# Where four small column sums stand in the first up projection of a transformer kernel

## The reference

```python
mod = silu(c) @ w_ada + b_ada                       # 6 * 1024 numbers
shift1, scale1, gate1, shift2, scale2, gate2 = split(mod, 6)
h = rms_norm(x, g_norm1) * (1 + scale1) + shift1
x = x + (1 + gate1) * (mixers(h) @ w_out)
h2 = rms_norm(x, g_norm2) * (1 + scale2) + shift2
u = causal_depthwise_conv(h2 @ w_up, w_conv, b_conv)    # w_up: 1024 x 5632, 3 taps
val, gte = split(u, 2)
x = x + (1 + gate2) * ((val * silu(gte)) @ w_down)      # w_down: 2816 x 1024
```

## Time and profile before

| | |
|---|---|
| median of 3 runs | 1052.29 us (1052.28 to 1053.61) |
| span of the profiled execution, first to last instruction | 1051.3 us |
| PE busy | 1020.2 us (97%) |
| DVE busy | 733.6 us (70%) |
| ACT busy | 562.0 us (53%) |
| share of PE in the chain that ended last | 87% |
| granted TensorE clock, mean | 0.997 of full speed |

### The profile page before, as it was taken

One profiled execution on the slowest core, in us unless ns is written; L12 is line 12 of the kernel. 1 busy time (PEld: TensorE's weight loads), 2 busy tenths in 40 slices (PEclk: granted clock), 3 DMA queues, 4 the chain that ended last, 5 costly groups with the idle time before them and its releaser, 6 DMA issues.

```text
span 1051.3 us, 22984 instructions
## 1 busy us (share of the span) xinstructions
PE 1020.2 (97%) x10004; PEld 966.9 (92%) x10004; DVE 733.6 (70%) x1194; ACT 562.0 (53%) x858; POOL 0.9 (0%) x7
## 2 busy tenths in 40 slices
PE   7999999999999999998999999999999999999996
PEld 6898889999999998986879999999888799999996
DVE  3898677899976667888557566566857665565654
ACT  4456474665565548764236444454667654444541
POOL 0000000000000000000000000000000000000000
PEclk9999999999999999999999999999999999999999
DMA  9978465466645553331005555465224435554541
GB/s 350 398 259 310 172 239 186 176 239 242 229 139 193 203 231 121 126 118 43 4 6 196 199 174 190 140 214 209 101 78 166 170 124 201 191 175 158 194 166 41
DMA packets 31236, 185.82 MB, mean 177 GB/s; under 512 B 3472, under 2 KB 4768, under 8 KB 13984
## 3 DMA queue, kind: packets, MB, share of 16 engines
q1 hardware_dynamic: 31136, 184.36, 49.2%
HBM read 183.29 MB, written 1.05 MB: 175 GB/s over the span
## 4 chain that ended last, share of the span: by engine, by line
PE 87%; DVE 5%; DMA 3%; ACT 3%; issue 1%; SPq 1%; DVEq 0%; ACTq 0%
PE banks L383 47%; PE banks L1390 17%; PE banks L348 3%; PE banks L380 2%; PE banks L660 1%; DMA land<-in_mkv_a 1%; DVE wlo L328 1%; PE banks L1933 1%; PE banks L1574 1%; PE banks L595 1%; PE banks L1923 1%; ACT whi L313 1%; PE banks L663 1%; DMA raw<-in_a_in 1%; DMA raw<-in_w_in 1%
## 5 line engine op out<-in xcount | busy, mean ns | idle before, releaser
L328 DVE TENSOR_TENSOR wlo<-raw,whi 128x2048 fp32r<-128x2048 f32 (+3 forms) x163 | 323.0, 1982 | 169.3 <-ACT whi L313 169.1
L313 ACT ACTIVATE whi<-raw 128x2048 fp32r<-128x2048 f32 (+3 forms) x163 | 270.7, 1663 | 107.4 <-PE banks L1390 73.5
L383 PE MATMUL banks<-h_lo,whi 128*128 128x256 f32 x1376 | 175.1, 279 | 0.0
L383 PE MATMUL banks<-h_hi,wlo 128*128 128x256 f32 x1376 | 173.1, 277 | 0.0
L383 PE MATMUL banks<-h_hi,whi 128*128 128x256 f32 x1360 | 172.1, 279 | 0.1
L383 PEld LDWEIGHTS banks<-h_lo,whi 128*128 128x128 f32 x1376 | 163.9, 187 | 3.2 <-issue 2.6
L383 PEld LDWEIGHTS banks<-h_hi,wlo 128*128 128x128 f32 x1376 | 163.8, 187 | 1.5 <-issue 1.2
L383 PEld LDWEIGHTS banks<-h_hi,whi 128*128 128x128 f32 x1360 | 162.1, 187 | 2.3 <-issue 1.2
L1416 ACT ACTIVATE u<-u 128x256 f32<-128x256 f32 x44 | 18.4, 418 | 124.9 <-DVE u L1470 124.9
L1390 PE MATMUL banks<-m_lo,whi 128*128 128x256 f32 x528 | 73.4, 278 | 0.0
L1390 PE MATMUL banks<-m_hi,wlo 128*128 128x256 f32 x528 | 73.2, 277 | 0.0
(11 more groups left out here) (453 smaller groups left out, 1408.8 us busy)
## 6 DMA issues: line engine op xcount, KB each, us to landing
raw<-in_ada SPq DMA_DIRECT2D x24, 1024.0 KB, 6.6
raw<-in_w_up SPq DMA_DIRECT2D x22, 1024.0 KB, 4.8
raw<-in_a_gu SPq DMA_DIRECT2D x22, 1024.0 KB, 4.8
raw<-in_b_gu SPq DMA_DIRECT2D x22, 1024.0 KB, 4.9
raw<-in_w_in SPq DMA_DIRECT2D x12, 1024.0 KB, 6.4
raw<-in_w_down SPq DMA_DIRECT2D x16, 704.0 KB, 4.1
raw<-in_a_in SPq DMA_DIRECT2D x11, 1024.0 KB, 6.3
raw<-in_a_down SPq DMA_DIRECT2D x16, 704.0 KB, 4.1
```

What stands on the lines that cost most here:

```text
L313: act.activation(hi_s[k % NSPLIT][:, 0:w], raw[n % NRAW][:, 0:w], ACT.Copy).then_inc(*hi_made.tick(k))
L328: dve.tensor_tensor(lo_s[s][:, 0:w], raw[n % NRAW][:, 0:w], hi_s[s][:, 0:w].bitcast(F), SUB).then_inc(*lo_made.tick(k))
L383: i_ = pe.matmul(b[0:m, j * T:(j + 1) * T], a[:, kt * step + j * m:kt * step + j * m + m], x[:, kt, :], start=st, stop=sp)
```

## The change

The four column sums 20 to 23 leave the places between two chunks (behind chunks 6, 10, 14 and 18) and go inside a chunk, behind its piece 3. The chunk is the first one from the old place on (`i >= 4 * n - 74`) that has buffer number zero: 7, 10, 16 and 19. Nothing else is touched; the number of instructions on each engine is the same.

```diff
+        ADA_UP = {}
+        for n in range(20, 24):
+            ADA_UP[min(i for i in range(4 * n - 74, 22) if split_k["w_up", i] % NSPLIT == 0)] = n
+
         def pe_ffn(pe, tag, up):
...
-                drain(pe_chunk(pe, up, i, b, h_hi, h_lo, 8, first=wait_h("n" + tag) if i == 0 else None,
-                               by_tile=PAIRED if i == 0 else ()))
-                if up == "w_up" and i % 4 == 2 and 2 < i <= 18:
-                    pe_ada(pe, 19 + i // 4)
+                for piece, _ in enumerate(pe_chunk(pe, up, i, b, h_hi, h_lo, 8, first=wait_h("n" + tag) if i == 0 else None,
+                                                   by_tile=PAIRED if i == 0 else ())):
+                    if up == "w_up" and piece == 3 and i in ADA_UP:
+                        pe_ada(pe, ADA_UP[i])
```

## The result

| | before | after |
|---|---|---|
| median of the runs (22 each) | 1053.51 us (1050.51 to 1058.62) | 1056.26 us (1051.46 to 1058.48) |
| span of the profiled execution | 1051.3 us | 1054.0 us |
| from the end of chunk 6 to `w_down` | 84.67 us | 85.82 us |
| from there to the next projection's first matmul | 61.06 us | 63.25 us |

The ratio is 1.0023, with a 95% interval of 1.0012 to 1.0034: slower by some 2.4 us, between 1.3 and 3.6. The 1052.29 us on which the prediction was built is the median of three of the 22 runs of before. Single runs of one kernel scatter over 7 to 8 us, so what follows is read from stages of the trace, of one profiled execution for each kernel.

The account below looks back on a forecast made before the run. PE was taken to bound the kernel. 18.4 more slow rows at 0.072 us (1.32 us), less two recovery rows of 0.018, gave +1.29 us: span 1051.3 to 1052.6, median 1052.29 to 1053.6 us; range 1050.9 to 1054.5 us.

Parts of the forecast that it names:

- PE alone sets the time here: Between 225 and 320 us the chain is PE alone, so every microsecond PE gains or loses moves the end.
- a sum ahead of the exit row spoils it: Up projection and `w_down` start: sums between `wlo0` and `whi0` prolong the slow pace; 35.4 slow rows against 17, +1.29 us.
- The prediction's count for the projection: Up projection: nine slow rows behind each of sums 20 to 22; behind 23, one of chunk 19, six of 20 and 21.
- Rival 1: The `h_lo` by `whi0` row ends the slow pace whatever precedes it: -1.22 us, 1051.1 us; chance 0.13.
- Rival 2: The slow pace survives pieces 4 and 5 but ends at the next chunk: -0.94 us, 1051.4 us; chance 0.16.
- The three sums that the prediction went by: Input projection, behind piece 3 in buffer zero: matmuls behind stayed at 281 ns, so the slow pace survives pieces 4 and 5.
- Rival 3: One pace everywhere: row distances have other causes, sums cost the same in both places, 1052.3 us; chance 0.06.
- the new wait: DVE idles about 4.2 us for sum 22; chunk 18's `wlo` ready near 290.1 us, PE waits for nothing.
- rival 4: The wait for sum 22 reaches PE at chunk 18; with DVE's backlog 3 us longer, 1055.0 us; chance 0.06.
- the slow pace ends in `w_down`: First half chunk of `w_down`: 22 slow matmuls (1.4 rows), then an exit at the passage from `wlo0` to `whi0`.
- rival 5: No exit in `w_down`: its other 506 matmuls and some 128 of the next projection slow, +4.1 us, 1056.4 us; chance 0.09.
- the level: Whole kernel: runs' median taken as 1.0 us above the profiled span, 1052.29 us before the change.

Follow-up runs that it names:

- experiment 2: The changed kernel with only sum 23 put back at its old place behind chunk 18; median 1054.44 us, ratio 0.9997 to before, second stage 61.05 us.
- experiment 5: The changed kernel with each sum one piece earlier, behind piece 2 of the same chunks; median 1053.12 us, ratio 0.9992 to before, projection 84.77 us.
- experiment 9: The changed kernel with the sums behind piece 1 of the same chunks; median 1052.46 us, ratio 0.9995 to before, projection 83.74 us.
- experiment 10: The changed kernel with the sums behind piece 0 of the same chunks; median 1052.10 us, ratio 0.9986 to before, projection 83.87 us.
- experiment 12: The changed kernel with every `wlo` 128 bytes off and sum 23 behind piece 3 of chunk 21; one run, 1051.63 us, second stage 61.23 us.
- experiment 6: The kernel before, sums untouched, with every `wlo` 128 bytes off; median 1053.52 us, ratio 0.9997 to before, projection 84.03 us.
- experiment 7: The kernel before with the 128-byte offset moved from `wlo0` to `wlo1`; one run, 1053.95 us, projection 84.88 us.
- experiment 8: The changed kernel with every `wlo` 128 bytes off; median 1052.85 us, ratio 0.9986 to before, projection 84.29 us, second stage 61.06 us.
- experiment 3: The changed kernel with the sums behind piece 3 of chunks 8, 11, 14 and 17, buffer number one; median 1054.69 us, ratio 1.0001 to before.

## Why the prediction was right and wrong

**Right: PE alone sets the time here, and the pace is what changes.** The projection is PE without a gap; the second stage has one wait, at its end, of 1.06 us before and 0.90 after. The clock is 1.00 in both.

**Right: a sum ahead of the exit row spoils it, and the slow pace survives pieces 4 and 5 and the step from buffer 0 to 1.** The prediction's count for the projection was 9 + 9 + 9 + 7 slow rows against 17, 17 x 0.072 = 1.22 us, less three recovery rows (one is left of four), 0.05 us: 1.17. Measured: 1.15. Rivals 1 and 2 are out by the rows at 231.40 and 233.37 us. The three sums that the prediction went by stood directly ahead of an exit, two behind a fast stream and one, at 156.17 us, behind a slow one (nine matmuls from 155.11 on, 117.8 ns each), as sums 21 and 23 do in the changed kernel. The fourth, which spoke against them, stood behind a slow stream and not ahead of an exit (shown under experiment 2); this difference was in the trace, and the prediction left it unread. Rival 3, one pace everywhere, is out too: over the kernels of this study the projection ran from 83.74 to 85.82 us with the same matmuls. The Trainium skill, "TensorE: Matmul & The Clock Gate", section "Part 2: What happens when you issue a matmul", speaks of reading weights beside a running matmul; its two ports may be as it says, but the two paces, 113.3 and 117.8 ns, show that one pace doesn't follow from them here.

**Right: the new wait.** DVE waited 4.32 us (4.2 predicted), the `wlo` of chunk 18 came at 290.6 us (290.1) and PE waited for nothing; rival 4 is out. Experiments 5, 9 and 10 leave sum 22 late (DVE waits 3.42, 2.51 and 1.60 us for it) and have projections 1.05 to 2.08 us shorter than the changed kernel.

**Wrong: the slow pace ends in `w_down`, behind its 22nd matmul.** This is the step that failed. The term was 1.4 rows, 0.10 us; it measured 2.19 us, 528 matmuls at 117.8 ns instead of 113.3 (2.4 us, of which 0.16 us is taken off the wait at the stage's end). This is rival 5, given 0.09. Its other part, 128 matmuls of the next projection, did not come: behind the wait of 0.90 us the pace was fast. Rival 5's 1056.4 us lies beside the measured 1056.26 by luck: its +4.1 us were 3.34 in the stages, and it stood on a level 1.2 us too low. The evidence was in the trace of before, in the third `w_down` above; I had looked for the slow pace only around the sums. The exit of the up projection was carried to rows of 11 in another loop, where nothing had shown one. Experiment 2 shows that sum 23 alone brings this term, experiment 12, in one execution, that even with the right addresses the first half chunk isn't an exit.

**Wrong: the level.** The forecast put its +1.3 us on 1052.29 us, the median of three runs; 22 runs give 1053.51. The 1.0 us between runs and span mixed two things: after, the profiled execution itself counted 1055.76 us at a span of 1054.0, 1.8 more, so the one that the prediction was read from stood near 1053.1 and not 1052.3. The level makes 1.2 us of the 2.7 between 1053.6 and 1056.26. `w_down` makes 2.1, and the two together are 0.6 more than is missing: the medians differ by 2.75 us where the two stages give 3.34, inside the interval of 1.3 to 3.6. The upper end of the range, 1054.5, is itself 0.25 above its own sum (1053.6 + 0.45 + 0.2 = 1054.25); the measured time lies above both. A kernel whose runs scatter over 8 us has no median known to 0.2% from three of them.

**Shown and open.** Shown, by moving and multiplying it: the exit is a passage from `wlo` to `whi` in a chunk whose `wlo` lies 128 bytes off modulo 256 from where the other buffers lie, in rows of 16 (experiments 6, 7, 8). Not separated: whether its distance from `whi` counts or its own address. Shown: a sum directly ahead of it (the changed kernel, 8), or eight matmuls ahead of it and out of a fast stream (5), spoils it; a sum 16 or 24 matmuls ahead, out of a fast stream, does not (9, 10). Open: what in the chip the two paces are; why a sum out of a slow stream is followed by the fast one in experiment 2 and at 146.00 us before, and by the slow one in the changed kernel; why a sum eight matmuls ahead of the exit spoils it only out of a fast stream (5); why `w_down` in rows of 11 went to its end without an exit. That short delays sometimes start the slow pace and sometimes don't, as at 987.33 us before and in the second or third `w_down` of experiments 3, 9 and 10 (61.86 to 61.95 us from the first matmul's start to the last one's, instead of 59.7 to 60.0), would account for some of the scatter of whole runs; no run tests how much.

## What to carry to other kernels

In a stream bound by TensorE, read the distance between starts, not durations or busy shares, and ask of every small matmul put into the stream how long the stream behind it runs differently, not only what it takes itself. When a forecast rests on how a state ends, look for that state through the whole trace, in every loop that it could reach, before pricing the end. Where whole runs scatter by more than the effect, compare the stages that the change touches.

## What the runs showed of the hardware

- Streams of 128x256 matmuls with a new weight each run at 113.3 or 117.8 ns a matmul, at one granted clock (1.00), and stay at one of the two for hundreds of matmuls (528 in `w_down`). The Trainium skill, "TensorE: Matmul & The Clock Gate", section "Back-to-back issue gap", gives the columns by 2.4 GHz plus 2.5 ns for an isolated gap at the full clock, by which 256 columns would take an estimated 109.2 ns, and says that in a stream of weight loads and matmuls both set the spacing, with 81 ns for 128 columns and 131 for 512. The streams of 256 columns here lie between those two, and none reached 109.2.
- Which of the two it is depends on what came before: in the first up projection the slow one began behind four short float32 matmuls (0.36 us in place) each time that the stream ahead was fast, and behind some delays of 0.1 us and not behind others (987.33 and 688.29 us before). Behind a wait of 0.90 us the fast one was back.
- Where the weights lie decides whether the slow pace ends: moving the 128 bytes, modulo 256, by which a `wlo` lies off the other buffers moved the exits from chunks 7, 13, 16 and 19 to 8, 11, 17 and 20 with not one instruction changed.
